# Swapping the two PSUM banks of the last two value tiles in a memory-attention step of a two-layer decoder trunk

## The reference

```python
z = x @ a_w_in[layer]
zu = gelu(z[..., :D_MIX])
zv = layer_norm(gelu(z[..., D_MIX:2 * D_MIX]), a_sgu_ln_g[layer], a_sgu_ln_b[layer])
qm = z[..., 2 * D_MIX:]
mix = chunked_sgu(zu, zv, a_w_s[layer], a_b_s[layer])      # gating over chunks of 128 tokens
...
mkv = mem @ mem_w_kv[layer]                                # 256 memory tokens, 4 heads of 64
p = softmax(qm @ mk.T / sqrt(64)); mo = p @ mv
y = concatenate([mix, mo]) @ w_o[layer]
x = layer_norm(DN_ALPHA * x + y, ...); x = layer_norm(DN_ALPHA * x + sq_relu_mlp(x, ...), ...)
```

## Time and profile before

| | |
|---|---|
| time, median of 3 runs | 1187.76 us (1186.54 to 1188.23) |
| profiled execution: time | 1186.62 us |
| its span | 1184.9 us |
| mean granted TensorE clock | 0.994 |
| TensorE busy | 1154.3 us, 97% of the span |
| VectorE busy | 632.8 us, 53% |
| ScalarE busy | 489.2 us, 41% |

### The profile page before, as it was taken

One profiled execution on the slowest core, in us unless ns is written; L12 is line 12 of the kernel. 1 busy time (PEld: TensorE's weight loads), 2 busy tenths in 40 slices (PEclk: granted clock), 3 DMA queues, 4 the chain that ended last, 5 costly groups with the idle time before them and its releaser, 6 DMA issues.

```text
span 1184.9 us, 16507 instructions
## 1 busy us (share of the span) xinstructions
PE 1154.3 (97%) x5840; PEld 970.4 (82%) x5840; DVE 632.8 (53%) x1080; ACT 489.2 (41%) x847; POOL 135.7 (11%) x156
## 2 busy tenths in 40 slices
PE   7989999999999999999999999999999999999997
PEld 7877789888888888889878888789888888888886
DVE  5667566644332444345578777866454323454226
ACT  5446236543211334224675555636543212333220
POOL 4200034200000000133400001035100000000000
PEclk9999999999999999999999999999999999999999
DMA  6521232333333333332311222123233333233232
GB/s 215 145 71 54 72 107 73 89 106 89 107 90 106 89 91 105 97 98 72 89 36 55 71 69 55 54 84 96 75 101 92 104 97 98 87 90 102 94 107 89
DMA packets 185591, 107.22 MB, mean 90 GB/s; under 512 B 4482, under 2 KB 180162, under 8 KB 185540
## 3 DMA queue, kind: packets, MB, share of 16 engines
q1 hardware_dynamic: 183236, 101.04, 29.3%
q10 hardware_dynamic: 2304, 5.51, 1.4%
HBM read 104.43 MB, written 2.10 MB: 90 GB/s over the span
## 4 chain that ended last, share of the span: by engine, by line
PE 80%; DVE 8%; ACT 4%; issue 4%; DMA 2%; POOL 1%; ACTq 0%; DVEq 0%; SPq 0%; POOLq 0%
PE proj L535 65%; PE pv L535 3%; PE sc L535 3%; DVE w_lo L1490 2%; PE proj L891 2%; PE tr L891 2%; PE pv L891 2%; PE tr L582 2%; PE sc L891 1%; ACT w_hi L1106 1%; DMA w_raw<-in_w_down 1%; ACT x L1276 1%; DMA mem_nat<-in_mem 1%; POOL total L2091 1%; DVE sc L1552 1%
## 5 line engine op out<-in xcount | busy, mean ns | idle before, releaser
L1490 DVE TENSOR_TENSOR w_lo<-w_raw,w_hi 128x1024 fp32r<-128x1024 f32 x171 | 217.8, 1273 | 164.6 <-ACT w_hi L1106 116.4
L535 PE MATMUL proj<-x_hi,w_hi 128*128 128x512 f32 (+1 forms) x768 | 300.3, 392 | 1.9 <-DVE w_lo L1490 0.7
L535 PE MATMUL proj<-x_hi,w_lo 128*128 128x512 f32 (+1 forms) x768 | 294.9, 385 | 0.0
L535 PE MATMUL proj<-x_lo,w_hi 128*128 128x512 f32 (+1 forms) x768 | 289.7, 384 | 0.0
L1106 ACT CAST w_hi<-w_raw 128x1024 fp32r<-128x1024 f32 x158 | 165.1, 1045 | 203.6 <-PE proj L535 197.9
L535 PEld LDWEIGHTS proj<-x_hi,w_hi 128*128 128x128 f32 x768 | 145.6, 190 | 30.2 <-ACT x_hi L1278 1.8
L535 PEld LDWEIGHTS proj<-x_hi,w_lo 128*128 128x128 f32 x768 | 145.5, 190 | 29.1
L535 PEld LDWEIGHTS proj<-x_lo,w_hi 128*128 128x128 f32 x768 | 143.1, 189 | 25.4
L535 PE MATMUL proj<-h_hi,w_hi 128*128 128x512 f32 (+1 forms) x384 | 146.4, 381 | 0.4 <-DVE w_lo L1490 0.4
L535 PE MATMUL proj<-h_hi,w_lo 128*128 128x512 f32 (+1 forms) x384 | 146.0, 380 | 0.0
L535 PE MATMUL proj<-h_lo,w_hi 128*128 128x512 f32 (+1 forms) x384 | 146.0, 380 | 0.0
(11 more groups left out here) (356 smaller groups left out, 1795.0 us busy)
## 6 DMA issues: line engine op xcount, KB each, us to landing
w_raw<-in_w_up SPq DMA_DIRECT2D x64, 512.0 KB, 4.0
w_raw<-in_w_down SPq DMA_DIRECT2D x64, 512.0 KB, 3.6
w_raw<-in_w_o SPq DMA_DIRECT2D x16, 512.0 KB, 3.6
w_raw<-in_a_w_in SPq DMA_DIRECT2D x14, 512.0 KB, 3.8
w_raw<-in_kv_w SPq DMA_DIRECT2D x12, 512.0 KB, 3.9
w_raw<-in_mem_w_kv SPq DMA_DIRECT2D x8, 512.0 KB, 4.5
w_raw<-in_b_w_q SPq DMA_DIRECT2D x8, 512.0 KB, 3.6
x_nat<-in_x ACTq DMA_DIRECT2D x2, 1024.0 KB, 11.6
```

The costliest lines, as they stand in the source:

```text
L535: last = pe.matmul(target, lhs, rhs, start=start and n == 0, stop=stop and n == len(terms) - 1)
L1490: return dve.tensor_tensor(target, whole, hi.bitcast(F32), ALU.subtract)
```

## The change

Tiles 4 and 5 change banks: tile 4 goes to `pv1` and tile 5 to `pv0`. The waits follow the new users of each bank. Tile 4 now waits for four copies (before: three) and for two finished heads (before: no such wait); tile 5 for three copies and three heads (before: four and four). In step 1, head 0 waits for three copies (before: five) and head 1 for five (before: four). The other tiles and step 0 keep bank and waits.

```diff
+    Z_BANK = [0, 1, 0, 1, 1, 0]
@@ turn_z(n), TensorE
-                wait(pe, z_out, n - 1)
-                if n in (2, 3, 5):
-                    pe.wait_ge(mix_ready, n - 1)
+                wait(pe, z_out, (0, 0, 1, 2, 4, 3)[n])
+                wait(pe, mix_ready, (0, 0, 1, 2, 2, 3)[n])
                 for t in range(TT):
-                    last = pe.transpose(pv[n % 2][:, t * P:(t + 1) * P], v_tmp[:, g.slot, t * P:(t + 1) * P], ident[:, :])
+                    last = pe.transpose(pv[Z_BANK[n]][:, t * P:(t + 1) * P], v_tmp[:, g.slot, t * P:(t + 1) * P], ident[:, :])
@@ attend(s, head), TensorE
-                    pe.wait_ge(z_out, (1, 2, 5, 4)[2 * s.base + head])
+                    pe.wait_ge(z_out, (1, 2, 3, 5)[2 * s.base + head])
@@ natural_z(n), VectorE
-                dve.tensor_copy(z_nat[:, :, n * P:(n + 1) * P], pv[n % 2][:, :].rearrange("p (t c) -> p t c", t=TT)).then_inc(z_out, 1)
+                dve.tensor_copy(z_nat[:, :, n * P:(n + 1) * P], pv[Z_BANK[n]][:, :].rearrange("p (t c) -> p t c", t=TT)).then_inc(z_out, 1)
```

## The result

| | before | changed |
|---|---|---|
| median | 1188.31 us (8 runs, 1186.54 to 1189.07) | 1181.37 us (8 runs, 1180.01 to 1184.63) |
| profiled execution: time, span | 1186.62, 1184.9 us | 1184.38, 1182.7 us |
| mean granted clock of that execution | 0.994 | 0.995 |

The ratio is 0.9948, with a 95% interval of 0.9936 to 0.9960: 6.2 us faster (4.8 to 7.6). The two medians are 6.94 us apart. The kernel is faster as forecast; the forecast time was 1182.6 us. The changed kernel's eight times stand in two groups, 1180.0 to 1181.9 (five) and 1184.4 to 1184.6 (three), and the profiled execution is one of the upper three. So the trace shown here needs two readings: what the change did, and why this execution was nevertheless only 2.2 us faster than the traced one of before.

The account below looks back on a forecast made before the run. TensorE, 80% of the chain that ends last, was taken to bound the kernel. The wait's 3.53 us and the clock's 1.58 make 5.11, from 1187.76 to 1182.6 us, range 1181.0 to 1185.0.

Parts of the forecast that it names:

- The wait, 3.53 us: Second memory step: head 0's product no longer waits for tile 4's copy and starts at 81.58 instead of 85.11.
- The clock, 1.58 us: Second memory step, product to next stage: the same work at full clock takes 6.74 instead of 8.32 us.
- the wait goes, the clock gives nothing: Rival, 18%: slow stretch missing in the timed runs of before, or another turns up elsewhere; time 1184.2 us.
- Step 0 as the template for step 1: The second memory step will follow the first's timeline, 24.28 us later, with 6.74 us from product to next stage.
- The softmax queue next, at no cost: Second turned tile: its normalization is there at 84.46, wanted at 84.69; cover 0.2 us, no loss taken.
- Tile 5's wait worth nothing, the other waits covered: Tile 5's wait had 0.54 us of cover, so easing it gains nothing; tile 4's and head 1's waits cost nothing.
- All of it reaches the end: Behind the second memory step: later waits keep their length, so the full 5.11 us reach the end.
- one of the signs named for being wrong: Rest of the span: the forecast is wrong if the late stages have moved by less than 5.1 us.
- The sum: Whole kernel: 5.11 us off the median of 1187.76 us gives 1182.6 us.
- Slower, by more slow stretches: Rival, 2%: later gaps fall under the slow clock, about 1.6 us a stretch; slower by over 0.2% from the fifth.

Follow-up runs that it names:

- the wait kept: The changed kernel with its new banks, but head 0 of the second step again waiting for five copies: ratio to before 0.9998.
- second changed: The changed kernel once more, unaltered: ratio to before 0.9951; six times, 1180.0 to 1185.5 us, the profiled execution 1181.7 us.
- second before: The kernel before once more, unaltered, one execution: 1188.9 us.
- the last four experiments: Changed kernel unaltered, 0.9951; changed kernel with three later gaps filled, 0.9939; kernel before with the same gaps filled, 0.9992; kernel before unaltered, 1188.9 us.

## Why the prediction was right

**The wait, 3.53 us.** Right. The two traces of the changed kernel have no such wait, and the run that put the one wait back lost the whole gain (0.9998). The reason given for its length, VectorE's queue, was right as well: a copy one place earlier in that queue shortened the wait to 1.77.

**The clock, 1.58 us.** Right, and it was the term with the most doubt. Filling the wait left the product where it was and gave 1.54 us. The rival "the wait goes, the clock gives nothing" has two halves. The first, that the slow stretch is missing in other runs of before, fell: behind the gap of 3.3 us the clock was at half in all four traces that have the gap idle (before twice, the wait kept, before with later gaps filled), and in none of the six without it (filled, shortened to 1.77 us, or gone). The second, that a stretch turns up elsewhere in its place, did happen in some executions: the upper group of times, from 1184.4 us, stands where this rival put it (1184.2), though for a stretch at 181 us that costs 2.6 and not 1.6.

**Step 0 as the template for step 1.** It gave 6.74 us from the product to the next stage; 6.75 was measured. Each of the forecast places came 0.1 us early, as the transposes themselves did.

**The softmax queue next, at no cost.** Right: there is no idle time ahead of either turned tile. The cover was as small as said: the last normalization ends at 84.01 + 0.35 = 84.36 and the turned tile starts at 84.59.

**Tile 5's wait worth nothing, the other waits covered.** Right; the trace of the run that leaves tile 5 in its bank has no wait there either, and the ratio of that run could not have told.

**All of it reaches the end.** In the first trace of the changed kernel it did not, and one of the signs named for being wrong came true: the late stages had moved by less. The 5.22 us gained ahead of 181 us were 2.58 at 598 us. The forecast had taken the rest of the span as unchanged, and there the clock was at half from 181 to 188 us. The other traces show that this stretch, and not a later wait, took the difference. The table gives the start of tile 4's transposes and of the transposes of the earlier trace rows in four pairs of traces, and how much of the distance between two kernels came in between:

| before / changed | tile 4's transposes | transposes near 598 us | gained between |
|---|---|---|---|
| first traces; only the changed one has the stretch | 81.23 / 81.13 | 598.27 / 595.69 | 2.48 us |
| first before, second changed; neither has it | 81.23 / 80.95 | 598.27 / 593.04 | 4.95 us |
| both with the gaps filled; neither has it | 81.50 / 80.78 | 598.97 / 593.10 | 5.15 us |
| second before, first changed; both have a long one | 80.63 / 81.13 | 600.23 / 595.69 | 5.04 us |

Where both kernels have the stretch, or neither, the step's 5.1 us arrive at 598 us. By TensorE's last matmul, near 1180 us, the last three pairs have gained 4.61, 5.52 and 5.01 us.

**The sum.** 5.11 us were forecast; it is 5.09 in the step and 6.2 (4.8 to 7.6) by the ratio. The mechanism and both terms are shown by the traces. That the time came out near 1182.6 is in part luck. The forecast took the median of three runs as the base, 1187.76, and over eight it is 1188.31; from there it would have been 1183.2, further from the measured 1181.37. And the median of a kernel whose times stand in two groups depends on how many fall in each: five of the first eight lay in the lower group, three of the six of the second run, and that median is 1183.50. The traced execution of before had escaped the stretch near 187 us; of the eight traces whose later gaps are not filled six have it, shorter or longer.

The ratio's middle lies 1 us above the step's 5.1, which is within its interval. The granted clocks of the timed runs suggest where more could come from. On the chip of the last four experiments its mean is 0.9929 over 17 runs of before and 0.9958 over 6 of the changed kernel, which is 16.9 and 9.8 us of the span at half clock. The slow stretch behind the stall accounts for about 3.5 of these 7.1 us (8.32 us at 0.79 in the earlier trace rows). So the changed kernel seems to meet less half clock elsewhere too. Why it would, no run here shows, and the clocks are on record to three digits only.

**Slower, by more slow stretches.** The mechanism named exists. It took back part of the gain in the traced run and, to judge by the times, in two of the other seven. The price given for a stretch, about 1.6 us, was too low for this long one (2.6), and the bound given, gaps of 2 us, was wrong: near 181 us the clock fell behind gaps of only 0.6 to 0.8 us close together, and with these filled it did not fall in either of two traces. That the gaps are the cause is likely from this, not settled: two of the eight traces with these gaps left as they are escaped too, and the times of before with the gaps filled are inconclusive. It did not decide, since the kernel before meets the same stretch.

## What to carry to other kernels

When two phases of one loop have the same instruction order and one stalls, lay their timelines side by side: here the offset between them priced the fix to 0.1 us, with the clock's part in it. A buffer whose writer stands right ahead of its next user on one engine, with another engine's queued copy between, should go to the other bank of the pair; which bank that is depends on who comes next, not on parity. Judge such a change by the length of its own stretch in the trace, because two executions of the changed kernel differ by up to 4.6 us (1180.01 and 1184.63), nearly all that the change is worth.

## What the hardware showed beyond expectation

A gap costs TensorE more than its length, but not always. Behind 3.28 us of idle TensorE the clock was at half in each of four traces, a loss of 1.5 us. Behind 1.77 us, in one trace, it was not. The page "TensorE: Matmul & The Clock Gate" of the Trainium skill, section "Part 1: The HAM clock gate", lets the number of slow matmuls vary from run to run; the traces agree for the later places (the stretch from 181 us in one trace of the changed kernel, none in the other), while the stretch behind the long gap came in all four traces that have this gap.

A slow stretch can also cost nothing. In the trace of before the clock is at half behind the gap that ends at 598.27; in the changed kernel's first trace the same gap, ending at 595.69, has full clock behind it (1.00 from 596 to 604 us). The changed kernel then waits where the other did not:

```profile
606.73 0.50 PE L536 MATMUL proj<-x_hi,w_hi 128*128 128x512 f32 x1 [1.57 <-DVE w_lo L1490]
```

That place is bound by VectorE, whose split of the weights comes at 605.45 in the changed kernel:

```profile
605.45 1.23 DVE L1490 TENSOR_TENSOR w_lo<-w_raw,w_hi 128x1024 fp32r<-128x1024 f32 x1
```

In before it comes at 608.09:

```profile
608.09 1.22 DVE L1490 TENSOR_TENSOR w_lo<-w_raw,w_hi 128x1024 fp32r<-128x1024 f32 x1
```

The difference is 2.64, practically the 598.27 - 595.69 = 2.58 from ahead of the slow stretch. TensorE's loss there lay under VectorE's work. The other traces agree: the three that have the slow stretch behind this gap lack the wait of 1.57 us, and the seven that do not have it show the wait.
